# Product with u in a PEER layer: one 512-column matmul for both activation parts, the two halves added on the way out

## What is computed

```python
q = (hf @ wq)                                   # 1024 -> 2048
s = einsum(q, keys)                             # scores against 128 keys per half and head
s1, i1 = top_k(s[.., 0], 16); s2, i2 = top_k(s[.., 1], 16)
sc, pos = top_k(s1 + s2, 16)                    # 16 experts per head and token
gate = softmax(sc)
act = gelu(einsum('td,ted->te', x, u_tab[e]))   # approximate=False
y = einsum('te,ted->td', gate * act, v_tab[e])
```

## Time and profile before

| | us |
|---|---|
| median of three runs | 3461.69 |
| the profiled execution | 3462.34 |
| its span, first to last instruction | 3460.6 |
| TensorE busy | 3242.6 (94% of the span) |
| VectorE busy | 2227.3 (64%) |
| ScalarE busy | 1665.9 (48%) |
| GpSimd busy | 153.1 (4%) |
| mean granted TensorE clock | 0.962 of full speed |

### The profile page before, as it was taken

How to read it: one execution, slowest core, us unless ns; L and a number is a source line. 1 busy time by engine, 2 the same in 40 slices (tenths; PEclk the granted TensorE clock), 3 DMA queues, 4 the chain that set the end, 5 groups by cost and what they waited for, 6 DMA issues and landing times.

```text
span 3460.6 us, 73223 instructions
## 1 busy us (share of the span) xinstructions
PE 3242.6 (94%) x25548; PEld 2866.2 (83%) x25548; DVE 2227.3 (64%) x4624; ACT 1665.9 (48%) x2924; POOL 153.1 (4%) x90
## 2 busy tenths in 40 slices
PE   8999999999999999999999898889889999669998
PEld 4899996588889999957888897877789999658887
DVE  6588947855556887497555672443348884785555
ACT  5544446744544444475455553222234444664454
POOL 0000000000000000000000362011100000000000
PEclk9999999999999999999999997998899999879999
DMA  8445454455564554544656441000145545115653
GB/s 317 170 170 182 164 187 146 134 194 194 194 208 163 182 181 171 176 136 156 218 192 205 150 140 56 3 2 2 49 146 182 182 170 182 36 62 193 206 193 134
DMA packets 143451, 530.29 MB, mean 153 GB/s; under 512 B 16544, under 2 KB 16688, under 8 KB 141040
## 3 DMA queue, kind: packets, MB, share of 16 engines
q1 hardware_dynamic: 141120, 514.01, 43.1%
q0 software_dynamic: 2224, 14.76, 1.2%
HBM read 522.42 MB, written 6.29 MB: 153 GB/s over the span
## 4 chain that ended last, share of the span: by engine, by line
PE 76%; DVE 11%; issue 7%; POOL 2%; ACT 2%; DVEq 1%; DMA 1%; ACTq 0%; SPq 0%; POOLq 0%
PE pS L1686 11%; PE pS L1688 11%; PE pS L1687 11%; PE pY L1815 10%; PE pY L1817 10%; PE pY L1819 10%; PE pY L1877 4%; PE pS L1877 3%; POOL lo L1562 2%; PE pG L1877 2%; DVE buf L1145 2%; DVE raw L1133 2%; DVE raw L1138 1%; PE pY L1719 1%; DVE gated L1138 1%
## 5 line engine op out<-in xcount | busy, mean ns | idle before, releaser
L1018 DVE TENSOR_TENSOR lo<-raw,hi 128x1024 fp32r<-128x1024 f32 x824 | 1009.7, 1225 | 787.3 <-ACT hi L541 784.0
L541 ACT CAST hi<-raw 128x1024 fp32r<-128x1024 f32 x872 | 913.1, 1047 | 520.4 <-PE pY L1819 505.6
L1686 PE MATMUL pS<-h_hi,hi 128*128 128x256 f32 x3552 | 1012.8, 285 | 32.7 <-DVE h_lo L1241 9.7
L1687 PE MATMUL pS<-h_lo,hi 128*128 128x256 f32 x3552 | 1007.7, 284 | 0.0
L1688 PE MATMUL pS<-h_hi,lo 128*128 128x256 f32 x3552 | 1007.6, 284 | 0.0
L1686 PEld LDWEIGHTS pS<-h_hi,hi 128*128 128x128 f32 x3552 | 684.5, 193 | 40.1 <-issue 27.4
L1687 PEld LDWEIGHTS pS<-h_lo,hi 128*128 128x128 f32 x3552 | 684.5, 193 | 0.2
L1688 PEld LDWEIGHTS pS<-h_hi,lo 128*128 128x128 f32 x3552 | 684.4, 193 | 0.0
L1815 PE MATMUL pY<-hi,h_hi 128*128 128x512 f32 x1536 | 473.7, 390 | 8.2 <-DVE h_lo L1169 8.2
L1817 PE MATMUL pY<-lo,h_hi 128*128 128x512 f32 x1536 | 473.8, 390 | 0.0
L1819 PE MATMUL pY<-hi,h_lo 128*128 128x512 f32 x1536 | 473.4, 389 | 0.0
(11 more groups left out here) (302 smaller groups left out, 3340.0 us busy)
## 6 DMA issues: line engine op xcount, KB each, us to landing
raw<-in_blocks SPq DMA_DIRECT2D x872, 512.0 KB, 3.3
gate_mod<-in_mod_wT SPq DMA_DIRECT2D x56, 512.0 KB, 3.5
raw<-in_mod_wT SPq DMA_DIRECT2D x20, 512.0 KB, 9.3
buf<-in_mod_wT SPq DMA_DIRECT2D x20, 512.0 KB, 8.1
buf<-in_keysT POOLq DMA_DIRECT2D x3, 1024.0 KB, 5.0
buf<-in_window SPq DMA_DIRECT2D x2, 1024.0 KB, 11.7
spill_x_res<-buf POOLq DMA_DIRECT2D x2, 1024.0 KB, 4.6
spill_x_h<-buf POOLq DMA_DIRECT2D x2, 1024.0 KB, 6.7
```

The source lines that it names most:

```text
L541: s.copy(hi[slot][:, :, :], raw[slot][:, :, :]).then_inc(hi_ready, 1)
L1018: v.tensor_tensor(lo[slot][:, :, :], raw[slot][:, :, :], hi[slot][:, :, :].bitcast(F32), ALU.subtract).then_inc(lo_ready, 1)
L1686: t_.matmul(out, hi[slot][:, c, :], h_hi[:, c, :], start=(c == 0), stop=False)
L1687: t_.matmul(out, hi[slot][:, c, :], h_lo[:, c, :], start=False, stop=False)
```

## The change

The three matmuls of a chunk become two. `h_hi` and `h_lo` become two halves of one tensor, `h_both`. The first matmul multiplies the high part of the weights by both, 512 columns wide, and fills a whole bank: columns 0 to 255 with high by high, 256 to 511 with high by low. The second adds low by high to columns 0 to 255. So the sum is left in two halves. ScalarE copies columns 256 to 511 to `buf`, VectorE adds columns 0 to 255 to it in place, and ScalarE applies Gelu in place one block later. Four banks are used in turn in place of two. The blocks of wq keep `s_block`. The diff:

```diff
-        h_hi = sb("h_hi", [P, NC, T], F32R)
-        h_lo = sb("h_lo", [P, NC, T], F32R)
+        h_both = sb("h_both", [P, 2, NC, T], F32R)
+        h_hi, h_lo = h_both[:, 0], h_both[:, 1]
...
+        u_banks = [pG[0], pG[1], pS[0], pS[1]]
...
+        half_copied = sem("half_copied")
...
+                def u_copy(n, b0, j):
+
+                    split_hi(n, k0 + NQ + b0, j + AHEAD)
+                    b = k0 + NQ + b0 + j + 1 + RING
+                    act.wait_ge(block_done, RING * n + b if n is not None else b)
+                    if n is not None or j:
+                        act.wait_ge(evacuated, RING * n + (2 + e0 + NQ + b0 + j) if n is not None else 2 + e0 + NQ + b0 + j)
+                    s.copy(buf[:, bass.ds(RING * n + (b0 + j), 1), :] if n is not None else buf[:, b0 + j:b0 + j + 1, :],
+                           u_banks[j % RING][:, T:2 * T].unsqueeze(1)).then_inc(half_copied, 1)
+
+                def u_gelu(n, b):
+
+                    x = buf[:, bass.ds(RING * n + b, 1), :] if n is not None else buf[:, b:b + 1, :]
+                    s.activation(x, x, ACT.Gelu)
+
                 def u_blocks(b0, nb):
-                    with act.Fori(0, nb // RING) as n:
+                    for j in range(RING):
+                        u_copy(None, b0, j)
+                        if j:
+                            u_gelu(None, b0 + j - 1)
+                    with act.Fori(0, nb // RING - 1) as n:
                         for j in range(RING):
-                            split_hi(n, k0 + NQ + b0, j + AHEAD)
-                            act.wait_ge(block_done, RING * n + (k0 + NQ + b0 + j + 1 + RING))
-                            s.activation(buf[:, bass.ds(RING * n + (b0 + j), 1), :], pS[j % 2][:, 0:T].unsqueeze(1), ACT.Gelu).then_inc(evacuated, 1)
+                            u_copy(n, b0 + RING, j)
+                            u_gelu(n, b0 + RING + j - 1)
+                    act.wait_ge(evacuated, 2 + e0 + NQ + b0 + nb)
+                    u_gelu(None, b0 + nb - 1)
+
...
+            def add_halves(n, g, b):
+
+                ve.wait_ge(half_copied, RING * n + (NE * g + b + 1) if n is not None else NE * g + b + 1)
+                x = buf[:, bass.ds(RING * n + b, 1), :] if n is not None else buf[:, b:b + 1, :]
+                v.tensor_tensor(x, u_banks[b % RING][:, 0:T].unsqueeze(1), x, ALU.add).then_inc(evacuated, 1)
+
...
                         route_unit(rt, n, j)
+                        add_halves(n, g, j)
...
                     st(g)
                     split_lo(None, ku + b, i + AHEAD)
+                    add_halves(None, g, b + i)
                 b += len(steps)
                 while b % RING:
                     split_lo(None, ku + b, AHEAD)
+                    add_halves(None, g, b)
                     b += 1
...
                         split_lo(n, ku + b, j + AHEAD)
+                        add_halves(n, g, b + j)
...
+            def u_blocks(k, e):
+                with pe.Fori(0, NE // RING) as n:
+                    for j in range(RING):
+                        slot = (k + j) % RING
+                        pe.wait_ge(lo_ready, RING * n + (k + j + 1 + RING))
+                        pe.wait_ge(evacuated, RING * n + (e + j + 3 - RING))
+                        out = u_banks[j]
+                        for c in range(NC):
+                            t_.matmul(out[:, :].rearrange("p (h t) -> p h t", h=2), hi[slot][:, c, :], h_both[:, :, c, :],
+                                      start=(c == 0), stop=(c == NC - 1), skip_group_check=True)
+                            mm = t_.matmul(out[:, 0:T], lo[slot][:, c, :], h_hi[:, c, :], start=False, stop=(c == NC - 1), skip_group_check=True)
+                        mm.then_inc(block_done, 1)
...
-                s_blocks(k0 + NQ, e0 + NQ, NE)
+                u_blocks(k0 + NQ, e0 + NQ)
 
                 pe.wait_ge(picks_ready, g + 1)
+                pe.wait_ge(evacuated, 2 + e0 + NQ + NE - 2)
```

## The result

The changed kernel takes 3514.17 us (median of 4 runs, 3511.61 to 3522.38), beside 3462.24 us for the kernel before in the same session (4 runs, 3461.26 to 3466.25). The ratio is 1.0152, with a 95% interval of 1.0133 to 1.0171. It is slower by 52 us where 12.6 us were forecast: the sign is right, and the time lies above the range. The profiled execution took 3511.61 us, with a span of 3509.8 us.

A forecast was written before the change was run, and what follows sets the result against it. TensorE was taken as the bound in routing and the last stretch, with VectorE nearly full in the steps. Terms 2.8 + 5.7 - 4.5 + 0.2 = +4.2 us per layer, +12.6 for three: 3474.3 us, range 3461 to 3498.

The forecast's parts named there:

- Routing: Routing stretch of u: VectorE becomes the bound, 16 rounds of 10.25 us plus four 0.34 us additions; +2.8 us per layer.
- That is all the room there is: Routing stretch: VectorE's 19.6 us of waits for ScalarE's casts in 64 blocks, 0.31 us per block, are its only room.
- The rule that was weighed: VectorE's additions: the skill's table charges PSUM operands 65 ns more, 0.405 us per addition, about +29 us in sum.
- Steps: Steps stretch: three waits vanish (-2.1), twenty additions (+6.8), later exponentials (+1.0); together +5.7 us per layer.
- rival 5: TensorE's clock falls after standing still some 5 us behind block 65; worst +3 us per layer, 3483 us; chance 0.02.
- The last 42 blocks: Last stretch of u: TensorE is the bound again, each 2.774 us block saving 0.107 us; -4.5 us per layer.
- Rival 2: The new TensorE block saves nothing, 2.88 us; +4.5 us per layer in the last stretch, 3488 us; chance 0.06.
- The end: End of u: block 127's copy and addition come ahead of VectorE's L1111; +0.2 us per layer.
- What was costed at nothing: ScalarE's extra copy, the new ring, the loads, the pick transposes and the rest of the kernel: no added time.
- rival 3: The ring of hand-overs between three engines binds, 0.3 us per block on top of VectorE's sum; 3530 us; chance 0.05.
- Rival 4: VectorE's addition costs only 0.20 us; -23 us in all, 3439 us; chance 0.19 together with a block under 2.67 us.
- Rival 1: VectorE's addition costs up to 0.42 us, as it waits on another engine's semaphore; +20 us, 3494 us; chance 0.16.

The follow-up runs named there:

- two-round body: The changed kernel with the addition right behind the low part, and VectorE's routing loop holding two rounds per pass, 8 passes for 16: 3494.05 us, ratio 1.0097.
- early addition: The changed kernel with the routing loop's addition issued right behind the low part instead of behind the quarter of the routing: 3502.19 us, ratio 1.0109.

## Why the prediction was wrong in size

**Routing, +13.5 us per layer where 2.8 stood: the step that failed.** It is "16 x (10.25 + 4 x 0.34)", and in it the 10.25 us. I measured it from a low part to the end of the last CAST of the round, and took what came between this CAST and the next low part for waiting on ScalarE, that is as room: "That is all the room there is". Of those 19.6 us, 7.7 were the loop's end on VectorE, about 0.5 us per pass, which no lateness of VectorE takes away. The two-round body showed it (0.52 us with a loop's end, 0.12 without), and the early addition's round adds up with it (12.12 for 11.94 to 12.17). Alone it is 16 x 0.5 = 8 us per layer.

The second half of the failure is the addition's hidden price. Its 0.34 us from the earlier trace rows was right wherever the loop stood; in the loop written out it was 0.24 us behind a MAX8. But that row has a constant address, and the addition in the loop takes its own from a register. Behind a short instruction that costs 0.12 us, in three slots of four, and at the loop's end both effects meet: 0.23 us ahead of the addition and 0.16 behind it. By rows: 11.61 + 3 x 0.12 + 0.23 + 0.16 = 12.36 us, against 12.20 to 12.40 measured. The two prices don't simply add up. With the address hidden behind a long instruction the loop's end cost the whole 0.5 us (early addition); with a constant address 0.1 to 0.2 us per round stayed over 11.61; with both in the way it is 0.6 to 0.8 us, some 11 us per layer, which is what the forecast lacks in routing.

**The rule that was weighed.** The trace shows no price for the PSUM operand: 256 elements with a PSUM operand took 425 ns in the loop (L1047) and 418 ns from SBUF alone (L1202), with 0.34 us to the next instruction. The Trainium skill ("VectorE: DVE Perf Modes", the table in "The TRN2 errata") would have 65 ns between them; the trace disagrees, so the measurement decides. That the sum of that rule, +29 us, was nearer to the result than mine is chance: the cause that it names isn't the one found here.

**Steps, +7.2 us where 5.7 stood.** VectorE at the start of the steps, first layer:

```profile
377.30 0.17 DVE L1228 COPY buf<-buf 128x16 f32<-128x16 f32 x1
...
382.11 1.23 DVE L1041 TENSOR_TENSOR lo<-raw,hi 128x1024 fp32r<-128x1024 f32 x1 [3.52 <-ACT hi L543]
```

The exponentials came 1.17 us later (4.81 us to the low part against 3.64), for 1.0 forecast. From the first low part of the steps to that of block 86 it is 68.13 us in the first layer, beside 62.11 before. Twenty additions of 0.34 us and the three waits of 2.07 us make 66.8 of it, and 1.3 us are left. In the first layer VectorE now waits 0.24 us for a cast and twice (0.54 us together) for a copy whose block TensorE has only just ended. TensorE had stood still for 5.0 us behind block 65, as rival 5 said, and came back at half clock, as the clock by stretch of 2 us shows (columns as in the earlier trace rows):

```profile
384.00:386.00 2.00, 2.00 (x8) 1.66 (x7) 1.90 (x5) 1.39 (x3) 0.00 (x0) 0.50 0.66 233
...
388.00:390.00 2.00, 2.00 (x13) 1.72 (x12) 1.93 (x5) 1.64 (x3) 0.00 (x0) 1.00 0.54 195
```

0.50 is the 1.2 GHz level, and before the gap and from 388 on it is 2.4 GHz. In the second layer the low clock lasted half as long, and the same stretch took 67.57 us, against 68.13 and 68.75 in the first and third. So 0.6 us of the 1.3 go with the longer half clock (1.2 us in the third layer); the rest was not taken apart. Rival 5 came true as a side effect, under the 3 us per layer that it allowed, and not as the case that decides.

**The last 42 blocks, -3.7 us where -4.5 stood.** The block was 2.773 us in two layers, the forecast to 1 ns, and 2.827 in the third. The sum of two measured distances, 226.7 + 120.1 ns, was right for the better pace, and nothing in the trace of before could show that there is a worse one. Rival 2 (2.88 us) is false.

**The end, +0.35 us where 0.2 stood.** VectorE reads the transposes behind block 127's addition:

```profile
569.00 0.42 DVE L1047 TENSOR_TENSOR buf<-pS,buf 128x256 f32 x1 [0.40 <-ACT buf L580]
569.34 0.68 DVE L1144 CAST raw<-pG 128x512 bf16<-128x512 f32 x1
```

The mechanism is as forecast, and the size is a little off.

**What was costed at nothing** holds. In routing VectorE never waits for the copy, so the ring of four banks doesn't bind (rival 3 false), and the earlier products of the kernel are unchanged. Rival 4, the cheap addition, is false for this kernel: no gap of the routing work was filled. Only in the loop written out did an addition fall to 0.24 us behind a MAX8, under the 0.29 us that rival 4 named as the point from which it decides. Rival 1 went the right way: in effect an addition cost some 0.5 us in routing. But it ended at 0.42 us, and its cause, the wait on a semaphore, is excluded by the run with the constant address, which kept the wait.

**What would have shown it.** Most signs that I named came: no waits for casts in routing, steps of about 73 us (74.2), blocks of 2.77 us (in two layers of three). TensorE stood still ahead of 41 to 43 of the 64 blocks of routing (over 0.15 us from one matmul to the next, where 0.12 is usual), less often than "nearly every block". The sign that failed was the round. I named "above 12 us" as the sign of the ring with waits for copy or casts; it came without them.

## What to carry to other kernels

A wait that ends "on" another engine is room only if that engine's instruction ended when the wait did: compare the two times before counting it, above all at a loop's end. Here they were 0.03 us apart where the wait was real, and 0.10 us or more where it was the loop. When an engine's queue is to become back to back, price its loop's end and its addresses out of registers; they cost nothing until then, and writing the loop out was worth 50 us here and nothing in the kernel before. A change that moves work from the bound to an engine with little slack belongs only in the stretches where that engine has the slack.

## What the hardware showed that I had not expected

- A loop's end on VectorE costs 0.40 us more than the same boundary inside the body (0.52 against 0.12 us). The trace books it as a wait for a cast of ScalarE that had been over: for 3.0 us in the two-round body, for 0.10 to 0.36 us in the first layer of the kernel before.
- An address out of a register costs VectorE 0.12 us behind an instruction of 0.06 us and nothing behind one of 1.23 us.
- With the loop written out an addition of 0.42 us added only 0.24 us between a MAX8 and the next low part (0.65 against 0.41 us).
- Alternating matmuls of 512 and 256 columns run at one of two paces, 346.6 or 353.3 ns per pair, at a clock of 1.00 in both; eight of one and then eight of the other gave 2.795 us per block each time.
- GpSimd's addition and a VectorE instruction on SBUF hold each other up, and the one that starts later pays: a low part of 1.23 us took 1.65 and a copy of 0.29 us took 0.84, while an addition of 0.74 us that started in a low part took 1.12.
